# Expert order by group, and a scatter-add written in two halves, in the routed mixture-of-experts stage of a two-block kernel

## The reference, cut to what matters

```
expert = g_idx * EXPERTS_PER_GROUP + e_idx          # 4 groups x 8 experts, top 2 inside the group
hid = silu(xb @ w_gate[e]) * (xb @ w_up[e])         # 1024 -> 256
y_rows = (hid @ w_down[e]) * row_w                  # 256 -> 1024
y = zeros.at[row_tok].add(y_rows)
x = x + gate2 * y
```

## Time and profile before

| | |
|---|---|
| three runs | 5118.76, 5118.84, 5122.7 us, median 5118.84 |
| the profiled execution | 5118.76 us |
| its span | 5117.0 us |
| PE busy | 4259.4 us, 83% |
| DVE, ACT, POOL busy | 2034.6, 1511.5, 604.5 us |
| mean granted TensorE clock | 0.91 |

### The profile page before, as it was taken

The page is one execution under the profiler, slowest core; times in us unless marked ns, Lnnn a source line. Parts: engine busy times, 40 slices in busy tenths (PEclk is TensorE's granted clock), DMA queues, the critical chain, the costliest instruction groups (busy, mean ns, idle before and its releaser), DMA issues. The chain is left out here.

```text
span 5117.0 us, 62169 instructions
## 1 busy us (share of the span) xinstructions
PE 4259.4 (83%) x19768; PEld 2793.9 (55%) x19769; DVE 2034.6 (40%) x4988; ACT 1511.5 (30%) x3300; POOL 604.5 (12%) x751
## 2 busy tenths in 40 slices
PE   3899997899676995589999979994988799279998
PEld 1667775788564452366776657772555444123333
DVE  0243434666775443701011137774323333323332
ACT  0122221454332331011111146653222122034443
POOL 0000000000231000010111000000000000323333
PEclk8999998999888997589999989996999899589999
DMA  8111111111444435075555232213110222078873
GB/s 303 38 59 49 59 49 58 45 43 32 141 146 159 144 123 206 29 254 170 185 174 191 72 107 64 65 50 108 51 51 9 94 103 97 21 288 293 292 244 70
DMA packets 284996, 605.81 MB, mean 118 GB/s; under 512 B 39896, under 2 KB 132312, under 8 KB 274608
## 3 DMA queue, kind: packets, MB, share of 16 engines
q1 hardware_dynamic: 230304, 416.27, 24.0%
q0 software_dynamic: 54544, 187.65, 12.2%
HBM read 457.94 MB, written 145.89 MB: 118 GB/s over the span
## 5 line engine op out<-in xcount | busy, mean ns | idle before, releaser
L1497 PE MATMUL out_psO<-out_w,out_mixT 128*128 128x512 f32 x1024 | 481.1, 631 | 18.7 <-DMA out_gr<-mod_out 17.1
L616 PE MATMUL inp_psU<-inp_w,inp_hT 128*128 128x256 f32 (+2 forms) x1440 | 443.0, 467 | 0.0
L616 PEld LDWEIGHTS inp_psU<-inp_w,inp_hT 128*128 128x128 f32 x1440 | 271.1, 190 | 158.6 <-issue 133.9
L1497 PEld LDWEIGHTS out_psO<-out_w,out_mixT 128*128 128x128 f32 x1024 | 207.3, 206 | 272.4 <-issue 253.4
L3258 PE MATMUL moe_psU<-moe_wu,moe_xT 128*64 x768 | 347.5, 606 | 2.6 <-issue 1.9
L3260 PE MATMUL moe_psU<-moe_bu,moe_xT 128*64 128x512 f32 x768 | 347.5, 606 | 0.0
L611 PE MATMUL inp_psU<-inp_hT,inp_w 128*128 128x256 f32 x1152 | 257.2, 384 | 34.3 <-ACT inp_fm L532 24.9
L611 PEld LDWEIGHTS inp_psU<-inp_hT,inp_w 128*128 128x128 f32 x1152 | 219.6, 192 | 67.8 <-ACT inp_fm L532 25.3
L2641 PE MATMUL inp_psU<-inp_hT,inp_w 128*128 128x256 f32 x1024 | 231.4, 383 | 15.0 <-DMA inp_wg<-in_lru_wx 15.0
L1925 PE MATMUL moe_psG<-moe_xT,moe_g_w 128*128 128x256 f32 x1024 | 234.5, 383 | 4.3 <-DMA moe_u_w<-in_w_up 4.3
L1941 PE MATMUL moe_psD<-moe_d_w,moe_hT 128*128 128x512 f32 x512 | 236.5, 622 | 0.9 <-DVE moe_hT L1980 0.9
(11 more groups left out here) (525 smaller groups left out, 7730.0 us busy)
## 6 DMA issues: line engine op xcount, KB each, us to landing
moe_wu<-in_w_up SPq DMA_DIRECT2D x32, 2048.0 KB
moe_g_w<-in_w_gate SPq DMA_DIRECT2D x16, 2048.0 KB
moe_u_w<-in_w_up SPq DMA_DIRECT2D x16, 2048.0 KB
moe_d_w<-in_w_down SPq DMA_DIRECT2D x16, 2048.0 KB
moe_wd<-in_w_down SPq DMA_DIRECT2D x32, 1024.0 KB
mod_mod_w<-in_w_mod SPq DMA_DIRECT2D x12, 2048.0 KB, 19.9
choose_mod_w<-in_w_ada SPq DMA_DIRECT2D x12, 2048.0 KB, 19.8
xn<-out_xn POOLq DMA_DIRECT2D x32, 512.0 KB, 3.8
```

Source lines behind the costliest of these rows:

```text
L616: mm = pe.matmul(psU[:, u % NB, 0:n], hT[:, par, k, j * P:(j + 1) * P], w[:, k, lo:lo + n], start=(k == 0), stop=(k == KD - 1))
L1497: mm = pe.matmul(psO[:, j, h, :], mixT[:, j, k, :], w[:, k, h * BANK:(h + 1) * BANK], start=(k == 0), stop=(k == KD - 1))
```

## The change

The experts are laid out in their own order: 8 of group 0, then 8 of group 1, and so on. The mask of the groups in `route_rows` and the three weight arrays follow. Now neighbouring blocks can belong to two experts of one group, so both halves of a unit may name the same output row. Therefore the put of a unit becomes two indirect DMAs of 64 rows (256 KB) each; the second waits until the first is stored, and the first waits until the second of the unit before is stored. A second table, `half_rows`, holds the row numbers of both halves on partitions 0 to 63; it is loaded by one more DMA in `route_rows`.

```diff
             pool.dma_start(row_table[:, :, :].rearrange("p b o -> p (b o)"),
                            table_dram.rearrange("(p b) o -> p (b o)", p=P)).then_inc(loaded, 16)
-            pool.wait_ge(loaded, 16)
+            pool.dma_start(half_rows[:, :, :, :].rearrange("r h b o -> r h (b o)"),
+                           table_dram.rearrange("(h r b) o -> r h (b o)", h=2, r=HALF)).then_inc(loaded, 16)
+            pool.wait_ge(loaded, 32)
...
-            ch.done(dve.tensor_scalar(out_g[:, :, :].rearrange("p t (n g) -> p t n g", g=G),
-                                      in_g[:, :, :].unsqueeze(2).to_broadcast([P, T, EG, G]), -1.0, None, ALU.add))
+            ch.done(dve.tensor_scalar(out_g[:, :, :].rearrange("p t (g n) -> p t g n", g=G),
+                                      in_g[:, :, :].unsqueeze(3).to_broadcast([P, T, G, EG]), -1.0, None, ALU.add))
...
             def put(u, p):
-                pool.tensor_copy(at_out[:, p, :], row_table[:, bass.ds(u, 1), 0]).then_inc(at_out_ready, 1)
-                pool.wait_ge(at_out_ready, u + 1)
-                pool.wait_ge(y_ready, u * 2 + 2)
-                if late(u, 1):
-                    pool.wait_ge(stored, u * 16)
-                pool.sem_inc(passed, 1)
-                pool.indirect_dma_start(out=out, out_offset=bass.IndirectOffsetOnAxis(ap=at_out[:, p, :], axis=0),
-                                        in_=y[:, p, :], in_offset=None, compute_op=ALU.add).then_inc(stored, 16)
+                for half in range(2):
+                    rows = slice(half * HALF, half * HALF + HALF)
+                    pool.tensor_copy(at_out[:, p, half, :], half_rows[:, half, bass.ds(u, 1), 0]).then_inc(at_out_ready, 1)
+                    pool.wait_ge(at_out_ready, u * 2 + (half + 1))
+                    pool.sem_inc(passed, 1)
+                    if half == 0:
+                        pool.wait_ge(y_ready, u * 2 + 2)
+                        pool.sem_inc(passed, 1)
+                    if late(u, 1) or half:
+                        pool.wait_ge(stored, u * 32 + 16 * half)
+                        pool.sem_inc(passed, 1)
+                    pool.indirect_dma_start(out=out, out_offset=bass.IndirectOffsetOnAxis(ap=at_out[:, p, half, :], axis=0),
+                                            in_=y[rows, p, :], in_offset=None, compute_op=ALU.add).then_inc(stored, 16)
...
                 if late(u, 2):
-                    dve.wait_ge(stored, u * 16 - 16)
+                    dve.wait_ge(stored, u * 32 - 32)
...
-    spread = np.arange(EXPERTS2).reshape(GROUPS2, -1).T.reshape(-1)
-    arrays["w_up_2"] = rows_apart(np.concatenate([I["w_gate_2"][0], I["w_up_2"][0]], 2)[spread])
-    arrays["w_down_2"] = rows_apart(I["w_down_2"][0][spread])
+    arrays["w_up_2"] = rows_apart(np.concatenate([I["w_gate_2"][0], I["w_up_2"][0]], 2))
+    arrays["w_down_2"] = rows_apart(I["w_down_2"][0])
```

More of the change, by code:

```diff
@@ L2931, in _, with route_rows @@
                 pool.wait_ge(stored[j], 16 * H * NT // 2)
-def route_rows(nc, K, logits, b_group, b_expert, table_dram, row_table, row_from, block_expert, block_slot, done_by):
+def route_rows(nc, K, logits, b_group, b_expert, table_dram, row_table, half_rows, row_from, block_expert, block_slot, done_by):
     T, E, G = SEQ // P, EXPERTS2, GROUPS2
@@ L3106, in _, with routed_experts @@
             ch.done(dve.tensor_scalar(done_by[:, :], done_by[:, :], 7, None, ALU.logical_shift_right))
-def routed_experts(nc, K, x_rows, row_table, row_from, block_expert, block_slot, done_by, w_up, w_down, scale2, shift2, gate_row, out):
+def routed_experts(nc, K, x_rows, row_table, half_rows, row_from, block_expert, block_slot, done_by, w_up, w_down, scale2, shift2, gate_row, out):
     name, FF, FB, NU, WB, XB = "moe2", FF2, FF2 // P, PAIRS2, SLOTS2, 4
@@ L3125, in routed_experts @@
         at = s.sb("at", [P, XB, 1], I32)
-        at_out = s.sb("at_out", [P, 2, 1], I32)
+        at_out = s.sb("at_out", [HALF, 2, 2, 1], I32)
         gc = s.sb("gc", [P, 2, 1])
@@ L3214, in _ @@
             put(NU - 1, 1)
-            pool.wait_ge(stored, 16 * NU)
+            pool.wait_ge(stored, 32 * NU)
         @block.tensor
@@ L3410, in hybrid_blocks @@
     row_table = nc.alloc_sbuf_tensor("row_table", [P, PAIRS2, 2], I32)
+    half_rows = nc.alloc_sbuf_tensor("half_rows", [HALF, 2, PAIRS2, 2], I32)
     row_from = nc.alloc_sbuf_tensor("row_from", [P, PAIRS2], I32)
@@ L3415, in hybrid_blocks @@
     table_dram = scratch("table", [P * PAIRS2, 2], I32)
-    route_rows(nc, K, lg3, A["b_router_group_2"], A["b_router_expert_2"], table_dram, row_table, row_from, block_expert, block_slot, done_by)
-    routed_experts(nc, K, xn3, row_table, row_from, block_expert, block_slot, done_by, A["w_up_2"], A["w_down_2"],
+    route_rows(nc, K, lg3, A["b_router_group_2"], A["b_router_expert_2"], table_dram, row_table, half_rows, row_from, block_expert, block_slot, done_by)
+    routed_experts(nc, K, xn3, row_table, half_rows, row_from, block_expert, block_slot, done_by, A["w_up_2"], A["w_down_2"],
                    columns(s22, 0, 0), columns(cols2, 24, 0), mod_row(mod2, 5), out)
@@ L3464 @@
     for n in ("b_mod", "b_ada_2", "b_gates", "q_norm_w", "k_norm_w", "sink", "mlstm_norm_w", "q_norm_2", "k_norm_2", "attn_out_norm_2",
-              "b_router_group_2"):
+              "b_router_group_2", "b_router_expert_2"):
         arrays[n] = I[n]
-    arrays["b_router_expert_2"] = I["b_router_expert_2"][:, spread]
     for n in ("conv_qk", "conv_w_2"):
@@ L3474 @@
     arrays["w_router"] = router(I["w_router"][0])
-    arrays["w_router_2"] = router(np.concatenate([I["w_router_group_2"][0], I["w_router_expert_2"][0][:, spread]], 1))
+    arrays["w_router_2"] = router(np.concatenate([I["w_router_group_2"][0], I["w_router_expert_2"][0]], 1))
     arrays["positions_2"] = column(I["positions_2"])
```

## The result

The changed kernel takes 5244.43 us (median of 4 runs, 5227.27 to 5247.15) against 5119.02 us before: ratio 1.0236, 95% interval 1.0213 to 1.0259. That is 125 us slower. The forecast was 5216 us, with 5155 to 5285 as the range.

What follows compares the result with a forecast made beforehand. PE bounds the kernel, losing 21.4 us to late weights. Thin experts first lose 35 us more, then the chain of half puts sets the pace: span 5213.6, plus 0.6 and 1.8, gives 5216 us; range 5155 to 5285.

Steps and rivals of the forecast that it cites:

- part 2: Last stage, puts in halves: from unit 12 the put chain sets the pace, 13.2 us a pair against PE's 11.69.
- the sum: Last stage's put chain: 36 pairs from 4733.5, 211 us beside loads and 263 us after, ending 5207.5; span 5213.6.
- the three waits: PE in the last stage before: waits for late weights, with half-clock stretches after them, lose 21.4 us.
- The counts of blocks: Blocks per expert from the reference's router: 79 in all, 40 units with work; thin groups 0 and 1 come first.
- Part 1: Last stage, expert order: thin experts first make weights late, 56 us lost by body 13, 35 us more than before.
- Two signs: POOL's landing waits grow from 168 to over 700 us; PE waits ahead of the down product in most units.
- Part 3: Routing and the rest: one more DMA issue on POOL, 0.6 us on the path; its landing at most 2 us.
- (a): Rival for the puts: a half costs about half, puts stay hidden, only part 1 counts; 5158 us, chance 0.20.
- (b): Rival for the puts: halves don't get cheaper than wholes, 13.7 us a pair after the loads; 5319 us, chance 0.13.
- (c): Rival for the weight loads: they speed up to 7.4 us an expert, also needing hidden puts; 5115 us, chance 0.03.
- (d): Rival for the order: it costs nothing because group 2's fat experts give time back; counted within anything else, 0.02.

Runs made afterwards that it cites:

- the order alone: Experts in their own order but whole puts, upper halves added into a scratch tensor, against the kernel before: 5150.87 us, ratio 1.0061.
- light loads: The changed kernel with the weight loads of experts 4 to 31 cut to 256 KB and 128 KB: 5143.72 us, ratio 1.0049 to the kernel before.
- the halves alone: The changed kernel with the experts back in the order of before, two serial half puts a unit: 5219.53 us, ratio 1.02 to the kernel before.
- the early load: Load of `wu` issued once the up products are made: kernel before 5097.72 us, order with whole puts 5126.72 us, changed kernel 5236.35 us.

## Why the prediction was right, and where its sizes were off

The mechanism was right in both parts. What failed is a piece of part 2: the sum let the puts set the time only from unit 12 on, as if nothing were queued by then; they were 11 us behind. That the total came close owes something to luck, as two sizes of a pair were off in opposite directions.

- **What bounds the stage before.** Right. PE is the bound, the three waits are the bare time from freeing a slot to landing: taking that away gave 22 us where the prediction counted 21.4.
- **The counts of blocks.** Right. The waits came in the bodies that the counts name, 9 and 10: 17.4 and 13.2 us in the change, 15.6 and 13.2 us with the order alone. Body 12, for which the count gave up to 4.4 us, waited 4.3 us with the order alone and 7.0 in the change.
- **Part 1, 35 us.** 31 us by the medians, 39 by the traces. The spacing of the loads was 14.8 to 14.9 us, not 13.2 (the upper bound was 14.4), which adds some 9 us by body 9. The bare wait with its half clock was smaller: from the transposes of h in body 9 (4661.61) to those in body 10 (4688.56) 27.0 us, so 15.3 over a body of 11.69, where I had 16.2 and 2.9. By body 13 the order alone had lost 60.6 us, where the sum had 56.
- **Part 2, the chain as the bound.** Right, and shown: 80 of 96 puts wait for a landing, a third `y` buffer gives nothing, and taking out the wait between the halves takes 84 of 100 us away.
- **The size of part 2.** From the earlier trace rows I had put a half at 4.7 us alone (a mean over both halves' issues) and 7.8 beside loads. Alone it is 4.7, in other parts than I thought: the issue of 64 rows takes 1.42 us, not 0.8, and what follows 3.3 us, 0.75 of the whole's 4.36. Beside back-to-back loads the slow half lands in about 9.2 us and the fast one, in the gap between two loads, in 4.7, so such a pair takes 15.3 us and not 17.4. The pairs of units 44 to 46 take 10.6 to 11.1 us, as the 11.0 of the sum, but those of units 33 to 43, with no load in flight and still gathers and copies beside them, take 12.4 on average, and 12.6 in the run with light loads. One size was too high and the other too low, and the mean pair from unit 12 on, 13.7 us against 13.2, came out near by luck.
- **Where the missing time lies.** In the profiled execution the first half of unit 12 is put at 4756.69; the sum said 4733.5. Of these 23 us, 1.7 were there when body 1 began (4525.33 against 4523.68), 4.6 are the order's own waits (60.6 against 56), 6 are later weights and lower clock in the changed kernel (66.6 us lost by body 13; until then neither PE nor VectorE waits for a put or a gather, and PE's waits for h are 49.0 us, 46.3 with the order alone), and 11 are the chain: it puts unit 12 24.5 us into body 13, where the sum had 13.5, because the pairs of units 10 and 11 took 24.1 and 16.5 us. Those 11 us the sum had at nothing. The 23 are the largest part of the 36 us by which the span exceeds the 5213.6 of the sum; the pairs after them added 15 us, and the end gave 3 back. The halves cost 93 us on top of the order alone, where the prediction had 62.
- **How the chain reaches PE.** Partly wrong. I wrote that `give` would hold PE and that the gathers have "a unit and more to spare". They haven't: with four buffers PE waits for gathered rows (25.2 us in 14 places, 41.2 with the halves alone), and VectorE for `y` in 7 places. Two signs that I named did not come: POOL's waits for landings rose to 335 us, not to over 700, and PE shows but 1.3 us of waiting ahead of the down product, though the bodies from 13 on are 14.0 us apart on average. With gathers further ahead all of it goes through `y`. The door changes, and it is not free: through `y` it was 39 us dearer, and there PE does stand still ahead of the down product (98 us in 30 places; the profile names no releaser for them).
- **Part 3.** The second table's load takes its place without a wait of its own: 0.67 us of issue, where 0.59 was counted, and the wait behind it is 1.66 us against 1.51 before.
- **The rivals.** (a), hidden puts, is out: a half alone takes 0.75 of a whole behind its issue, not 0.5, and even with light loads the kernel takes 5144 us. (b), halves not cheaper, is out: it had 5319 us. For the slow half beside a load alone it is nearly true: behind its issue it takes 7.8 us of the 8.9 that a whole takes. (c), faster loads, is out: they came slower, 14.8 us apart. (d), an order that costs nothing, is out by the 31 us of the order alone.
- **The fixed part.** By the Trainium skill, "DMA: Bandwidth & Descriptors", section "Anatomy of one DMA — SWDGE (gpsimd) path", 2.0 us of a DMA are fixed and the rest goes by bytes; worked out from the whole's 5.92 us, a half alone would be an estimated 4.0 us, and 4.7 were measured. The measurement decides: halving an accumulating scatter saved 1.2 of 5.9 us. The estimate of a pair beside loads by that page, 15.6 us, is nearer to the measured 15.3 than my 17.4.

What stays open: how much of a slow landing beside loads is the gather behind the half and how much its place against the weight loads, and how much of the early load's lost gain in the change is slower landings and how much the chain's own length.

## What to carry to other kernels

A chain in which each DMA waits for the landing of the one before costs its landings. Cut each link in two and it pays 1.6 times as much alone (10.6 to 11.1 us a pair against 6.8 for a whole) and 1.2 times beside loads (15.3 against 12.8), and it becomes the bound as soon as one pair of landings exceeds the body of the pacing engine. Before giving up a data layout that makes rows distinct, price the waits it saves: here the layout of before was worth 100 us in waits and 31 us in when weights are due (39 by the traces). And when weights come late, look at what frees their buffer: releasing the part that is done first gave 22 us with no other change.

## What the runs showed of the hardware that was not expected

- The issue of an accumulating indirect DMA hardly shrinks with the rows: 1.56 us for 128 rows of 4 KB, 1.42 us for 64.
- The time from issue to landing beside weight loads was not one value: 4.7 us for the half in the gap between two loads, about 9.2 us for the one in a load's stream with the gather behind it, for the same 256 KB. Without the loads, gathers still there, the longest was 6.8 us.
- Freeing a buffer by a landing can line up two things that were apart before. With the gathers further ahead, VectorE's copy and POOL's issue started together in nearly every unit and the issue went from 1.45 to 3.34 us.
